# Gate and decay columns as one block of the projection, and the log gates of all tiles made during it

## The reference, cut to what matters

```python
def ab_prepare(t, w_in, conv_w, a_log, dt_bias, gla_gate_w, gla_gate_b):
    gq, gk, gv, gz, ga, gb, lq, lk, lv, lg, llr = jnp.split(t @ w_in, AB_SPLITS, axis=-1)
    ...
    gate = jnp.einsum('bldr,drk->bldk', heads(llr, 2, GLA_GATE_RANK), gla_gate_w) + gla_gate_b
    return dict(
        ...
        gdn_g=-jnp.exp(a_log) * jax.nn.softplus(heads(ga, 2, GDN_HEADS) + dt_bias),
        gdn_beta=jax.nn.sigmoid(heads(gb, 2, GDN_HEADS)),
        gla_log_a=(jax.nn.log_sigmoid(gate) / GLA_GATE_TAU).reshape(b, l, 2, GLA_HEADS, GLA_DK), ...)

def run_gla(q, k, v, log_a, s0, emit):
    bc = jnp.cumsum(log_a, axis=-2)
    kd = k * jnp.exp(bc[..., -1:, :] - bc)
    ...
```

## Time and profile before

| | us |
|---|---|
| runs, median of 3 | 3971.87 |
| lowest, highest | 3965.63, 3974.07 |
| the profiled execution, its own time | 3979.76 |
| its span in the trace | 3978.0 |
| its granted clock of TensorE, mean of the span | 0.981 |

### The profile page before, as it was taken

The page is one execution under the profiler, slowest core; times in us unless marked ns, Lnnn a source line. Parts: engine busy times, 40 slices in busy tenths (PEclk is TensorE's granted clock), DMA queues, the critical chain, the costliest instruction groups (busy, mean ns, idle before and its releaser), DMA issues.

```text
span 3978.0 us, 47344 instructions
## 1 busy us (share of the span) xinstructions
PE 3883.1 (98%) x19506; PEld 3212.9 (81%) x19506; DVE 2056.6 (52%) x2946; ACT 1326.3 (33%) x1979; POOL 500.3 (13%) x526
## 2 busy tenths in 40 slices
PE   8999999999999989999999989999999999999999
PEld 5788988788878878888888867888888888778887
DVE  6636555746548985334443554433643344543345
ACT  3335443322233333223322354322432233332233
POOL 0025542100012220002100143000100000010001
PEclk9999989999999999999999999999999999999999
DMA  6220003446231114233232321332323233012322
GB/s 217 84 70 1 1 1 96 149 148 192 80 114 47 61 48 134 85 102 100 90 102 86 102 64 47 98 104 80 111 93 98 84 98 98 21 64 90 106 88 71
DMA packets 342992, 350.73 MB, mean 88 GB/s; under 512 B 9723, under 2 KB 338235, under 8 KB 342524
## 3 DMA queue, kind: packets, MB, share of 16 engines
q1 hardware_dynamic: 342780, 347.71, 27.4%
...
## 4 chain that ended last, share of the span: by engine, by line
PE 82%; DVE 3%; ACT 1%; issue 1%; POOL 0%; DVEq 0%; ACTq 0%
PE ps L378 23%; PE ps L379 23%; PE ps L380 23%; PE ps L1576 2%; PE ps L2531 1%; PE ps L3610 1%; PE ps L2569 1%; PE ps L3597 1%; PE ps L385 1%; PE ps L2552 1%; PE ps L3580 1%; PE ps L3111 1%; PE ps L2939 1%; DVE wlo L360 0%; PE ps L466 0%
## 5 line engine op out<-in xcount | busy, mean ns | idle before, releaser
L360 DVE TENSOR_TENSOR wlo<-raw,whi 128x2048 fp32r<-128x2048 f32 (+6 forms) x305 | 622.0, 2040 | 881.2 <-ACT whi L354 881.1
L378 PE MATMUL ps<-Xh,whi 128*128 128x512 f32 x2632 | 1034.7, 393 | 4.8 <-ACT cr L2718 2.5
L380 PE MATMUL ps<-Xh,wlo 128*128 128x512 f32 x2632 | 1026.0, 390 | 0.0
L379 PE MATMUL ps<-Xl,whi 128*128 128x512 f32 x2632 | 1025.8, 390 | 0.0
L354 ACT ACTIVATE whi<-raw 128x2048 fp32r<-128x2048 f32 (+6 forms) x305 | 514.6, 1687 | 1073.7 <-PE ps L380 1066.0
L378 PEld LDWEIGHTS ps<-Xh,whi 128*128 128x128 f32 x2632 | 495.2, 188 | 112.8 <-issue 9.3
L379 PEld LDWEIGHTS ps<-Xl,whi 128*128 128x128 f32 x2632 | 495.2, 188 | 103.6 <-issue 1.7
L380 PEld LDWEIGHTS ps<-Xh,wlo 128*128 128x128 f32 x2632 | 495.0, 188 | 103.6
L378 PE MATMUL ps<-HDh,whi 128*128 128x512 f32 x1056 | 411.7, 390 | 0.0
L380 PE MATMUL ps<-HDh,wlo 128*128 128x512 f32 x1056 | 410.9, 389 | 0.0
L379 PE MATMUL ps<-HDl,whi 128*128 128x512 f32 x1056 | 410.8, 389 | 0.0
...
## 6 DMA issues: line engine op xcount, KB each, us to landing
raw<-in_ffn_w SPq DMA_DIRECT2D x44, 1024.0 KB, 5.4
raw<-in_ffa_w_gate_up SPq DMA_DIRECT2D x44, 1024.0 KB, 5.1
raw<-in_ffb_w_gate_up SPq DMA_DIRECT2D x44, 1024.0 KB, 5.0
mslot<-in_mod_w SPq DMA_DIRECT2D x28, 1024.0 KB, 8.1
raw<-in_mod_w SPq DMA_DIRECT2D x20, 1024.0 KB, 6.1
raw<-in_ab_w_in SPq DMA_DIRECT2D x14, 1024.0 KB, 5.3
...
raw<-in_hy_w_in SPq DMA_DIRECT2D x12, 1024.0 KB, 5.2
```

The costliest lines, as they stand in the source:

```text
L360: dve.tensor_tensor(k.part(k.wlo, c), k.raw(c), k.part(k.whi, c).bitcast(F32), ALU.subtract).then_inc(*k.ev.put("dve_wlo", ("lo", n), ("ra ...
L378: pe.matmul(o, wh, xh, start=first, stop=False)
L379: pe.matmul(o, wh, xl, start=False, stop=False)
L380: return pe.matmul(o, wl, xh, start=False, stop=last)
```

## The change

1. gab and llr become one block `glx` of 64 columns (16 of gab, 16 of zeros, 32 of llr), laid out by the host as an array of its own, in the place that gab had. The block llr at the end of the projection is gone. DVE reads both halves of glx out.
2. The GDN gates are made within the projection: gab's transposes on PE behind lq, their steps on ACT and DVE behind lq and lk, `cc` on PE behind the first half of lv.
3. The log gates of all six tiles are made within the projection, in two batches of three: tiles 4, 5, 0 behind lq (PE), ending on DVE behind lk; tiles 3, 1, 2 behind the first half of lv, ending on DVE behind its second chunk step. Each is one product over 512 columns (both directions). SP stores them in DRAM (`la_gates`), and in the scan loads the two halves that tile j needs into one of two buffers `lab`. The step `lla` of the scan does nothing any more.
4. Memsets move from the joint into the scan: POOL's of ub, SL, atE and atO to steps 4 and 8 of the row, of OG and OL to steps 120 and 160, DVE's of dq to step 100.
5. The sums of modulation chunks 9, 10 and 11 have buffers of their own. DVE reads the result of chunk 8 at the step of chunk 10, and those of 9 to 11 in the joint.

```diff
-AB_PARTS = (("qkv", 0, 1536), ("gab", 2048, 16), ("lq", 2064, 256), ("lk", 2320, 256), ("lv", 2576, 512),
-            ("llr", 3600, 32))
+AB_PARTS = (("qkv", 0, 1536), ("glx", 0, 64), ("lq", 2064, 256), ("lk", 2320, 256), ("lv", 2576, 512))
...
-    lin_pe(k, pe, "gab", keys_of("gab", 16), 8, k.X7, lambda kk: (), W2, after=side)
+    lin_pe(k, pe, "glx", keys_of("glx", 64), 8, k.X7, lambda kk: (), W2, after=side)
     late_pe(k, pe, 11)
     lin_pe(k, pe, "lq", keys_of("lq", 256), 8, k.X7, lambda kk: (), after=side)
+    gates_pe(k, pe)
+    la_pe(k, pe, 0)
     lin_pe(k, pe, "lk", keys_of("lk", 256), 8, k.X7, lambda kk: (), W2, after=side)
-    lintok_pe(k, pe, "lv", keys_of("lv", 512), 8, k.X7, 6, after=lambda i: steps())
-    lin_pe(k, pe, "llr", keys_of("llr", 32), 8, k.X7, lambda kk: (), W2)
-    mod_fin_pe(k, pe, MODS_PROJ - 2)
+
+    def behind(i):
+        steps()
+        if i == 0:
+            la_pe(k, pe, 1)
+            cc_pe(k, pe)
+        else:
+            mod_fin_pe(k, pe, MODS_PROJ - 2)
+    lintok_pe(k, pe, "lv", keys_of("lv", 512), 8, k.X7, 6, after=behind)
...
+LA_TILES = ((4, 5, 0), (3, 1, 2))
...
+def la_pe(k, pe, b):
+
+    if b == 0:
+        pe.wait_ge(*k.ev.at(("in", "gw")))
+    for t in LA_TILES[b]:
+        ps = room(k, pe, ("la", t))
+        pe.matmul(ps[:, :], k.llr[:, tok(t)], k.gw[LLR, :], start=True, stop=True).then_inc(
+            *k.ev.put("pe_prep", ("mm", "la", t)))
+
+
+def cc_pe(k, pe):
+
+    pe.wait_ge(*k.ev.at(("in", "ums")))
+    pe.wait_ge(*k.ev.at("g"))
+    ps = room(k, pe, ("cc",))[:, 0:96].rearrange("p (f d t h) -> p f d t h", f=2, d=2, t=6)
...
+def la_abs_dve(k, dve, b):
+
+    if b:
+        dve.wait_ge(*k.ev.at(("la stored", 0)))
...
+def la_store_sp(k, sp, b):
+
+    for i, t in enumerate(LA_TILES[b]):
+        sp.wait_ge(*k.ev.at(("la", t)))
+        sp.dma_start(k.lad[t], k.lax[i][:, :]).then_inc(*k.ev.put("d_la_out", *([("la stored", b)] if i == 2 else []), n=16))
+
+
+def la_load_sp(k, sp, j):
+
+    if j > 1:
+        for x in ("bc", "kd"):
+            sp.wait_ge(*k.ev.at(("mm", x, j - 2)))
...
-    steps = Steps(lambda *a: mod_dve(k, dve, *a), 0, MODS_PROJ)
+    def mod_step(x, *_):
+        if 0 < x < MODS_PROJ - 3:
+            mod_fin_dve(k, dve, x - 1)
+        elif x == MODS_PROJ - 2:
+            mod_fin_dve(k, dve, x - 2)
+        mod_sum_dve(k, dve, x)
+    steps = Steps(mod_step, 0, MODS_PROJ)
...
     for i, key in enumerate(keys_of("lv", 512)):
         steps()
         next_lo(k, dve, key)
+        if i == 0:
+            la_abs_dve(k, dve, 1)
+    la_dve(k, dve, 1)
+    cc_dve(k, dve)
+    dve.wait_ge(*ev.at(("la", LA_TILES[1][0])))
     mod_sum_dve(k, dve, MODS_PROJ - 1)
-    plain_dve(k, dve, "llr", 0, 32)
-    mod_fin_dve(k, dve, MODS_PROJ - 2)
...
-    if s == "lla":
-        act.wait_ge(*ev.at(("la2", j)))
-        act.activation(k.la2[:, :], k.la2[:, :], ACT.Exp, scale=-1.0).then_inc(*put("act_gla"))
-        act.wait_ge(*ev.now())
-        act.activation(k.la2[:, :], k.la2[:, :], ACT.Ln, bias=1.0).then_inc(*put("act_gla", ("lsp", j)))
-    elif s == "lbc":
+    if s == "lbc":
...
     gdn_early_sp(k, sp)
+    upto(("mod", 9), 0)
+    la_store_sp(k, sp, 0)
     upto(("z0", 0), 0)
+    la_store_sp(k, sp, 1)
     gdn_sp(k, sp)
```

More of the change, by code:

```diff
@@ L1219, in proj_pe, with gates_pe @@
-    lin_pe(k, pe, "llr", keys_of("llr", 32), 8, k.X7, lambda kk: (), W2)
-    mod_fin_pe(k, pe, MODS_PROJ - 2)
-    k.ev.also(("end", "proj", "pe"))
+    def behind(i):
[6 more added lines that the diff above has]
+    lintok_pe(k, pe, "lv", keys_of("lv", 512), 8, k.X7, 6, after=behind)
+    k.ev.also(("end", "proj", "pe"))
+LA_TILES = ((4, 5, 0), (3, 1, 2))
+def gates_pe(k, pe):
+    ev = k.ev
+    ps = room(k, pe, ("gab cols",))
+    for t0, n in W2:
+        pe.wait_ge(*ev.at(("out", "glx", 0, t0)))
+    for t in range(6):
+        ins = tr(k, pe, ps[:, t * 16:t * 16 + 16], k.gab[:, tok(t)])
+    ins.then_inc(*ev.put("pe_prep", ("mm", "gab cols")))
@@ new lines, in la_pe @@
+def la_pe(k, pe, b):
[9 more added lines that the diff above has]
+    ps = room(k, pe, ("cc",))[:, 0:96].rearrange("p (f d t h) -> p f d t h", f=2, d=2, t=6)
+    for f in range(2):
+        for d in range(2):
+            ins = pe.matmul(ps[:, f, d], k.Ums[:, 2 * f + d, :], k.gx[:, :, 4 * d:4 * d + 4], start=True, stop=True)
+    ins.then_inc(*k.ev.put("pe_prep", ("mm", "cc")))
@@ new lines, in gates_exp_act @@
+def gates_exp_act(k, act):
+    ev = k.ev
+    act.activation(k.al, k.col("alog", 0, 8), ACT.Exp).then_inc(*ev.put("act_prep", "al"))
+    act.wait_ge(*ev.at("gx0"))
+    pv = k.bk.of(("gab cols",))[:, 0:96].rearrange("p (t c) -> p t c", t=6)
+    act.activation(k.bx[:, :, :], pv[:, :, 8:16], ACT.Exp, scale=-1.0).then_inc(*ev.put("act_prep", "bx0", ("out", "gab cols")))
+    act.wait_ge(*ev.at("gx1"))
+    act.activation(k.spl, k.spl, ACT.Exp, scale=-1.0).then_inc(*ev.put("act_prep", "spl exp"))
@@ new lines, in la_abs_dve @@
+def la_abs_dve(k, dve, b):
+    if b:
+        dve.wait_ge(*k.ev.at(("la stored", 0)))
+    for i, t in enumerate(LA_TILES[b]):
+        dve.wait_ge(*k.ev.at(("mm", "la", t)))
+        dve.tensor_tensor(k.lax[i][:, :], k.bk.of(("la", t))[:, :], k.col("glab", 0, 512), ALU.add).then_inc(
+            *k.ev.put("dve_prep", ("out", "la", t)))
+        dve.wait_ge(*k.ev.now())
+        dve.scalar_tensor_tensor(k.lae[i][:, :], k.lax[i][:, :], -1.0, k.lax[i][:, :], ALU.mult, ALU.max).then_inc(
+            *k.ev.put("dve_prep", ("la abs", t)))
@@ L1848, in gdn_dve @@
+    made = {("OG", 0): "OG zero", ("OG", 1): "OG zero", "OL": "OL zero"}
+    for n, (d, hp, j, s, part) in enumerate(scan_order()):
+        if n == 100:
+            dve.memset(k.dq[0][:, :, :, :], 0.0)
+            dve.memset(k.dq[1][:, :, :, :], 0.0).then_inc(*ev.put("dve_prep", "dq zero"))
         if d is not None:
```

239 lines of the change are left out of this document (131 added, 108 removed).

## The result

| | before | after |
|---|---|---|
| runs, median (lowest to highest), us | 3971.07 (3965.63 to 3974.07), 4 runs | 3944.81 (3943.14 to 3950.0), 4 runs |
| ratio, 95% interval | | 0.9938 (0.9922 to 0.9954) |
| profiled execution, own time / span | 3979.76 / 3978.0 | 3943.14 / 3941.3 |
| granted clock, mean of the span | 0.981 | 0.987 |

The account below looks back on a forecast made before the run. TensorE (PE), busy 98% of the span, was taken as the bound. Terms of - 8.3 + 7.1 + 5.0 + 2.0 - 2.0 - 5.0 - 7.0 - 2.0 + 1.0 = - 9.2 us, from the median 3971.9, gave 3963; range 3951 to 3977.

Parts of the forecast that it names:

- Part 1: End of the projection: the block llr's 48 products leave PE's path, minus 8.3 us.
- Part 2: Projection: PE gains gab transposes, cc and six log-gate products in two batches of 2.8 us, plus 7.1.
- Part 3: Projection, before cc: PE waits for DVE behind chunk 9's late load, plus 5.0 us; lower clock after it, plus 2.
- Part 4: Joint and scan's start: eR gains 3.1 us, POOL's chain with ub memsets up to 1 later; net minus 2.
- Part 5, waits and products: Scan after 286.4 us: products gone, minus 5.0; PE's waits gone, minus 7; new memsets, plus 1.
- Part 5, clock: Scan: two half-level clock stretches that followed log-gate waits go, 1.7 us each, taken as minus 2.
- the waits move on: Rival, scan: PE meets the next waiter, so minus 7 and minus 2 fall away; 3972 us, chance 0.17.
- the scan gives more: Rival, scan: clock holds where PE ran 20.5 us at half level; 8 us more, 3955; chance 0.15.

Follow-up runs that it names:

- e8: Kernel before with only gab and llr merged into block glx, the block llr gone; gates and log gates stay in joint and scan: 3957.92 us, ratio 0.9972.
- e6: Changed kernel with its memsets put back where they stood, in the joint: 3940.09 us, ratio 0.9926 to the kernel before.
- e1: Kernel before with Exp in place of Ln in the scan's log gates, so no ACT table loads in the scan: 3955.56 us, ratio 0.9964.
- e2: Kernel before with ACT taken out of the scan's log gates, DVE's three steps and PE's products kept: 3947.99 us, ratio 0.9942.
- e7: Changed kernel with modulation chunk 9 loaded ahead of the first stores and chunk 8's result read before the second log-gate batch: 3945.57 us, ratio 0.9935.
- e9: Kernel before with its ring of seven banks moved on six places at the scan's start, as in the changed kernel: 3965.26 us, ratio 0.9986.
- e10: Changed kernel with its ring of seven banks moved on one place, back to that of the kernel before: 3947.31 us, ratio 0.9947.
- e4: Changed kernel with the log gates made in the scan again, tile by tile, other parts kept: 3967.73 us, ratio 0.9999 to the kernel before.
- e3: Changed kernel with ACT's Exp and Ln put back at each tile's lla as mere load, result not awaited: 3949.78 us, ratio 0.9951.
- e5: Changed kernel with ACT's Exp and Ln put back at each tile's lla, PE's lbc products waiting for them: 3950.28 us, ratio 0.9951.
- e11: Changed kernel with chunk 9 first, memsets back in the joint, and ub's memsets ahead of POOL's waits for masks and lvm: 3934.61 us, ratio 0.9916.

## Why the prediction was wrong

The direction and most mechanisms were right; the time, 3944.8, lies below the range of 3951 to 3977. Two things failed: the term for the clock in part 5 (minus 2, where the clock loss of the whole kernel fell by 7.9 us although two new stretches cost about 5), and a term that the sum did not have, the ring of banks (3.3 to 4.1 us at full clock). By its own steps:

- **Part 1** (llr, minus 8.3): the products left, but e8 shows that alone they would bring 3.5 us before 3255 at full clock, as PE then waits 4.2 us for DVE's sums. In the change, with PE slowed by parts 2 and 3, nothing of that wait is seen. The term was right for the whole change.
- **Part 2** (two batches of 2.8): 2.81 and 2.84 us. Right.
- **Part 3** (wait plus 5.0, clock plus 2.0): cc began at 250.10, inside the predicted 249.6 to 251.6. The wait was 3.07 because PE came later, slowed by a half-level stretch from 208.4 to 211.8 right behind the first batch, where before there was none. With that and 6.9 us at the half level from 249.3 the place costs 3.1 + 1.7 + 3.4 = 8.2 us against 7.0.
- **Part 4** (minus 2 in all: 3.1 won in the joint, about 1 lost behind eR): eR stood at 274.73, as predicted. The joint gave 2.7 us. From eR to the first product with kdt it took 19.48 us before and 18.70 after, so 0.8 more was won: minus 3.5 in all. But before, 17.1 us of that start ran at the half level, after it 10.2; at full clock nothing is won there. I had seen that ub's and SL's memsets lie in POOL's chain, but trusted POOL's room: PE waited 3.7 us for POOL's BT. For the whole move of the memsets the traces of e6 have 2.6 us lost, where I had about 1 at the start and 1 in the scan.
- **Part 5, waits and products** (minus 5, minus 7, plus 1): from 292 to 600 us the changed kernel gained 11.7 us at full clock, predicted 11. The sum fits better than its parts: PE's busy time at full clock fell by 6.8 us (predicted 5) and its idle time by 4.9 (predicted 6, with the memsets). Its named waits went, la's 2.4 and most of those for ACT, but those for DVE's XX rose by 2.4: a part of what the rival "the waits move on" had. e1 adds what I did not single out: the table loads alone carry half of it.
- **Part 5, clock** (minus 2): here the step failed. It counted two stretches that follow one long wait each. Over the executions the clock loss fell by 7.9 us, though by the profile the projection's new stretches added about 5; so what parts 4 and 5 cover gave about 13. e2 has a fall of 13 from ACT's part of the log gates alone. The rival "the scan gives more" was the nearest one. But its price of 8 us rests on the stretch of 20.5 us, and that stretch is one draw, present in three profiles of thirteen (before, e7, e9), in e7 without log gates in the scan. That the fall over the executions is of the same size is luck.
- **What no step held**: the ring of banks, 6.7 us in the traces, 3.3 of them at full clock (3.6 and 4.1 in the means of e9 and e10). The prediction never asked what the change moves behind the scan.
- **Sum at full clock**: predicted minus 9.2 (the clock terms, plus 2 and minus 2, cancel). By the trace the start has 0.0 (predicted plus 1.8), the scan minus 11.7 (minus 11), the ring minus 3.3: minus 14.9. By the runs it is minus 16.0. With the clock's 7.9 that makes the 24.

What stays open is why the clock loss is 58 to 65 us in the kernels with the awaited log gates in the scan (before, e4, e8, e9), 57 without the loads (e1), and 50 to 57 in those without (e2, e3, e5 to e7, e10, e11). The border is thin: e8's 58.0 is not clear of the 57, and e8 is 5 below before with all its log gates in the scan. The waits that the log gates cause go with the loss, but e3 added waits without adding loss, so how much PE waits in the scan does not settle it. That the log gates' place changes the loss is shown by e2 and e4; how it does is not.

The Trainium skill, "ScalarE: Activation LUTs", section "What ACT_TABLE_LOAD costs", adds a drain to each switch; in the changed kernel, too, the next ACTIVATE stands 0.01 us behind the load (276.11, 1.28, 277.40), so the traces again do not show it.
